# Two weight slots filled once ahead of the experts, and 4 MB loads from the third pair of experts on

## The reference, cut to what matters

```python
def moe(h, w_router, b_router, w_gate, b_gate, w_up, b_up, w_down, b_down):
    logits = (t @ w_router + b_router).astype(jnp.float32)
    top_v, top_i = lax.top_k(logits, TOP_K)
    ...
    for e in range(N_EXPERTS):
        gate = jnp.minimum(t @ w_gate[e] + b_gate[e], SWIGLU_LIMIT)
        up = jnp.clip(t @ w_up[e] + b_up[e], -SWIGLU_LIMIT, SWIGLU_LIMIT)
        hid = (up + 1.0) * gate * jax.nn.sigmoid(gate * SWIGLU_ALPHA)
        y = y + comb[:, e:e + 1] * (hid @ w_down[e] + b_down[e]).astype(jnp.float32)
```

## Time and profile before

| | us |
|---|---|
| three runs | 1310.83, 1312.16, 1315.89 |
| median | 1312.16 |
| span of the profiled execution | 1309.2 |
| TensorE busy in it | 1268.5 |

### The profile page before, as it was taken

One profiled execution on the slowest core, in us unless ns is written; L12 is line 12 of the kernel. 1 busy time (PEld: TensorE's weight loads), 2 busy tenths in 40 slices (PEclk: granted clock), 3 DMA queues, 4 the chain that ended last, 5 costly groups with the idle time before them and its releaser, 6 DMA issues.

```text
span 1309.2 us, 18733 instructions
## 1 busy us (share of the span) xinstructions
PE 1268.5 (97%) x8160; PEld 623.4 (48%) x8160; DVE 412.6 (32%) x836; ACT 192.1 (15%) x353; POOL 16.8 (1%) x38
## 2 busy tenths in 40 slices
PE   9999999999999999999999999999899999999996
PEld 7778765677763443434434343433334343443332
DVE  4987745433122122131222212122122212122122
ACT  4114322221121010000100000010000000010002
POOL 0002000000000000000000000000000000000000
PEclk9999999999999999999999999999999999999998
DMA  9335041495989999999999999999999999999995
GB/s 320 129 111 133 4 138 59 161 377 227 421 323 412 427 428 426 429 427 429 429 429 435 430 432 432 429 430 430 432 430 433 433 433 433 433 433 432 423 427 197
DMA packets 33955, 464.41 MB, mean 355 GB/s; under 512 B 7824, under 2 KB 9424, under 8 KB 13024
## 3 DMA queue, kind: packets, MB, share of 16 engines
q1 hardware_dynamic: 33056, 459.53, 84.3%
q0 software_dynamic: 832, 3.90, 0.9%
HBM read 458.34 MB, written 5.07 MB: 354 GB/s over the span
## 4 chain that ended last, share of the span: by engine, by line
PE 75%; DMA 22%; DVE 2%; ACT 1%; issue 0%; SPq 0%; DVEq 0%
PE ps L1191 37%; PE ps L613 25%; DMA arena<-in_w_down 10%; DMA ring<-in_w_down 9%; PE ps L1222 4%; PE ps L1267 2%; DMA ring<-in_w_gate 2%; PE ps L1218 1%; PE ps L1204 1%; PE ps L1210 1%; DVE ring L1600 0%; DMA ring<-in_w_in 0%; PE ps L1312 0%; PE ps L1255 0%; PE ps L1269 0%
## 5 line engine op out<-in xcount | busy, mean ns | idle before, releaser
L1191 PE MATMUL ps<-ring,xT 128*64 128x512 f32 x1536 | 341.7, 595 | 2.0 <-DMA ring<-in_w_gate 1.3
L613 PE MATMUL ps<-arena,ring 128*128 128x288 f32 (+3 forms) x1136 | 225.3, 366 | 1.2 <-DMA ring<-in_w_in 1.1
L1191 PEld LDWEIGHTS ps<-ring,xT 128*64 128x64 f32 x1536 | 106.2, 137 | 227.2 <-issue 217.3
L613 PEld LDWEIGHTS ps<-arena,ring 128*128 128x128 f32 (+1 forms) x1136 | 176.6, 177 | 47.5 <-issue 4.7
L1191 PE MATMUL ps<-ring,arena 128*64 128x512 f32 x768 | 171.7, 596 | 7.7 <-DMA ring<-in_w_down 7.7
L1355 ACT ACTIVATE arena<-ps 128x512 f32<-128x512 f32 (+5 forms) x136 | 76.4, 570 | 634.4 <-PE ps L1210 367.3
L1191 PE MATMUL ps<-arena,xT 128*64 128x512 f32 x512 | 114.7, 595 | 0.0
L1191 PEld LDWEIGHTS ps<-ring,arena 128*64 128x64 f32 x768 | 52.9, 137 | 108.5 <-issue 97.9
L2063 DVE TENSOR_TENSOR arena<-arena,ps 128x512 f32<-128x512 f32 x64 | 44.0, 688 | 130.2 <-PE ps L1267 117.3
L2015 DVE TENSOR_TENSOR xT<-ps,vec 128x1024 f32<-128x1024 f32 x15 | 18.4, 1225 | 177.7 <-PE ps L1222 177.7
L1191 PE MATMUL ps<-arena 128*64 128x512 f32 x256 | 61.5, 624 | 11.5 <-DMA arena<-in_w_down 11.5
(11 more groups left out here) (227 smaller groups left out, 771.9 us busy)
## 6 DMA issues: line engine op xcount, KB each, us to landing
ring<-in_w_up SPq DMA_DIRECT2D x18, 4096.0 KB, 29.5
ring<-in_w_up SPq DMA_DIRECT2D x28, 2048.0 KB, 21.9
ring<-in_w_down SPq DMA_DIRECT2D x14, 4096.0 KB, 30.8
ring<-in_w_gate SPq DMA_DIRECT2D x9, 4096.0 KB, 30.2
arena<-in_w_gate SPq DMA_DIRECT2D x9, 4096.0 KB, 29.2
ring<-in_w_down SPq DMA_DIRECT2D x16, 2048.0 KB, 20.1
ring<-in_w_gate SPq DMA_DIRECT2D x14, 2048.0 KB, 21.4
arena<-in_w_gate SPq DMA_DIRECT2D x14, 2048.0 KB, 24.9
```

The lines of the kernel that those rows point to most:

```text
L613: return nc.tensor.matmul(out, lhsT, rhs, start=start, stop=stop)
L1191: last = nc.tensor.matmul(out[AT[h ^ swap], :], lhs(k), part(weights(i), 0, 4, D)[:, k % 4, h * 512:(h + 1) * 512], start=(fresh and k == ...
```

## The change

Eight slots stay in turn, and two more, 8 and 9, are placed at the end of a longer `arena`. They take the first two loads of the first pair and are not refilled with weights. Each other load keeps its number; as `FIRST_SLOT` goes, load L stands in slot L % 8. [...] The four large conv stores are issued in two halves each. The matrix whose loads are cut into pieces in the first pair is n = 5 in place of n = 4, and the pieces follow product 1. `small` keeps two biases; the rest is `small_later`, in the second pair, behind `up_done` 2. `WHOLE` becomes 1: loads of 4 MB from the third pair on, and the down biases are added there.

```diff
-WHOLE = 3
+WHOLE = 1
...
-FIRST_SLOT = 2
+ONCE = 2
...
-    return (FIRST_SLOT + load) % SLOTS, load // SLOTS
+    return load % SLOTS, load // SLOTS
+
+
+def place_first(n, c):
+
+    load = 2 * n + c
+    return (SLOTS + load, 0) if load < ONCE else place(0, n, c)
...
+LATER_FILLS = [f - (i < ONCE) for i, f in enumerate(FRONT_FILLS)]
...
-        arena = sb("arena", [P, 23224])
+        SPARE = 27096 - ONCE * SLOT
+        arena = sb("arena", [P, 27096])
...
-            last_front = [("wo_ps", 4), ("wo_ps", 8)] + [("sv_ps", n + 1) for n in range(4)] + [("sv_ps", 4), ("o_out", XH)]
+            last_front = [("wo_ps", 4), ("wo_ps", 8)] + [("sv_ps", n + 1) for n in range(4)] + [("sv_ps", 4), ("o_out", XH)] + [("sk_ps", 4)] * ONCE
 
             def small():
+                for dst, name in ((b_gate, "b_gate"), (b_up, "b_up")):
+                    sp.dma_start(dst, A[name]).then_inc(S["ext_ld"], 16)
+
+            def small_later():
+                sp.wait_ge(S["up_done"], 2)
+                sp.dma_start(b_down, A["b_down"]).then_inc(S["ext_ld"], 16)
                 sp.dma_start(gf_row, A["g_final_row"].broadcast_to([P, D])).then_inc(S["ext_ld"], 16)
                 for d in range(4):
                     sp.dma_start(gf_tail[TAIL * d:TAIL * (d + 1)], A["g_final_row"][:, 256 * d:256 * (d + 1)].broadcast_to([TAIL, 256])).then_inc(S["ext_ld"], 16)
-                for dst, name in ((b_gate, "b_gate"), (b_up, "b_up"), (b_down, "b_down")):
-                    sp.dma_start(dst, A[name]).then_inc(S["ext_ld"], 16)
...
                 for n, (w, p) in enumerate(MATRICES):
+                    if second and n == 2:
+                        small_later()
                     for c in range(2):
-                        i, fill = place(odd, n, c)
-                        if first and fill == 0:
+                        i, fill = place_first(n, c) if first else place(odd, n, c)
+                        if first and n < 5:
                             sem_, val = last_front[i]
                             sp.wait_ge(S[sem_], val)
-                        elif not (first and n == 4):
+                        elif not first:
...
-                        elif first and n == 4:
+                        elif first and n == 5:
                             for k in range(4):
                                 if k < 3:
                                     sp.wait_ge(S["first_k"], 3 * c + k + 1)
+                                elif c == 0:
+                                    sp.wait_ge(slot_free[i], emptied(odd, n, c)[1])
                                 else:
-                                    sp.wait_ge(slot_free[i], emptied(odd, n, c)[1])
+                                    sp.wait_ge(S["up_done"], 1)
...
-            experts(1, 1, 0, 1)
-            with sp.Fori(1, WHOLE) as t:
-                for odd in range(2):
-                    experts(2 * t + odd, 2 * t + odd, t, odd)
+            experts(1, 1, 0, 1, second=True)
...
-                pool.dma_start(O["conv"][:, c, 1:, :],
-                               ext[:, c, TAPS - 1 + SEQ:].rearrange("p (b t) -> p b t", b=NB)[:, :, NT:]).then_inc(S["conv_sent"], 16)
+                for b in range(0, NB, NB // 2):
+                    pool.dma_start(O["conv"][:, c, 1 + b:1 + b + NB // 2, :],
+                                   ext[:, c, TAPS - 1 + SEQ:].rearrange("p (b t) -> p b t", b=NB)[:, b:b + NB // 2, NT:]).then_inc(S["conv_sent"], 16)
...
-                    if opening and n == 0 and k % 4 < 3:
+                    if opening and n == 1 and k % 4 < 3:
                         last.then_inc(S["first_k"], 1)
...
-    nc = bacc.Bacc("TRN2", target_bir_lowering=False, num_devices=1)
+    nc = bacc.Bacc("TRN2", target_bir_lowering=False, num_devices=1, dynamic_dma_scratch_size=1024)
```

More of the change, by code:

```diff
@@ L93, in halves_left_out @@
     return (PAIRS // 2 - 1 - WHOLE) * sum(per_pair) + per_pair[0]
+LATER_FILLS = [f - (i < ONCE) for i, f in enumerate(FRONT_FILLS)]
 FREED = [sum(frees(n, c) for odd in range(2) for n in range(6) for c in range(2) if place(odd, n, c)[0] == i)
          for i in range(SLOTS)]
+UNFREED = [sum(frees(load // 2, load % 2) for load in range(ONCE) if load == i) for i in range(SLOTS)]
 def emptied(odd, n, c):
@@ L106, in emptied @@
         at = 6 * odd + n - 4
-        return "slot_free", sum(frees(m, c) for o, m in loads if 6 * o + m <= at) + (0 if at >= 0 else 0)
+        return "slot_free", sum(frees(m, c) for o, m in loads if 6 * o + m <= at) - UNFREED[i]
     done = "up_done" if n_was in (1, 3) else "down_done"
@@ L169, in weights @@
         def weights(i):
-            return ring[:, i * SLOT:(i + 1) * SLOT] if i < RING else arena[:, (i - RING) * SLOT:(i - RING + 1) * SLOT]
+            if i < RING:
+                return ring[:, i * SLOT:(i + 1) * SLOT]
+            at = (i - RING) * SLOT if i < SLOTS else SPARE + (i - SLOTS) * SLOT
+            return arena[:, at:at + SLOT]
         def whole_slot(i):
@@ L191, in build @@
         shift_out = sb("shift_out", [P, RW, 1 + NB])
-        amax = sb("amax", [P, 9])
-        asum = sb("asum", [P, 9])
+        amax = const[:, 1230:1239]
+        asum = const[:, 1240:1249]
         hT = part(arena, 0, KT, TOK)
@@ L228, in build @@
         sq_tail = arena[:, 10496:10752]
[L229 to L233, removed]
+        gf_row = arena[:, SPARE:SPARE + D]
+        b_gate = arena[0:NE, 13056:14080]
+        b_up = arena[NE:2 * NE, 13056:14080]
+        b_down = arena[0:NE, SPARE + D + 256:SPARE + 2 * D + 256]
+        gf_tail = arena[:, SPARE + D:SPARE + D + 256]
         h_tail = arena[0:2 * TAIL, 14080:14592]
@@ L240, in build @@
         combT = arena[0:NE, 18240:18528]
[L241 to L244, removed]
+        one_e = part(arena, 12928, 2, CAP)[0:2 * NE]
+        pick = part(arena, 10752, TT, 2, CAP)
+        wpick = part(arena, 11136, TT, 2, 2, CAP)
+        ye = (arena[:, 11904:12416], arena[:, 12416:12928])
         after_x = xT[:, :, :].rearrange("p k t -> p (k t)")
@@ L248, in build @@
         y_out = (after_x[:, 2048:3072], after_x[:, 0:1024])
[L249 to L254, removed]
+        w_r = part(arena, 18528, KT, NE)
+        b_r = const[:, 640:672]
+        logit = part(const, 672, TT, NE + TOPK)
+        top8 = part(const, 780, TT, 8)
+        others = part(const, 804, TT, NE + TOPK)
+        dummy = eps[:, 2:3]
         dummy_ln = part(scratch, 13550, 1)
         sqsum = arena[:, 14336:14336 + TOK]
[L257 to L263, removed]
+        mask = part(const, 912, TT, NE)
+        comb = part(const, 1008, TT, NE + 2)
+        pos = part(const, 1110, TT, NE + 2)
+        esum = const[:, 1212:1215]
+        ntop = const[:, 1215:1218]
+        ssq = const[:, 1218:1221]
+        sqx = part(arena, 10752, KT, TOK)
         rstd = ssq
-        load = arena[:, 19856:19857]
-        sq_half = arena[:, 19812:19816]
-        sq_bias = arena[:, 19816:19818]
+        load = const[:, 1221:1222]
+        sq_half = const[:, 1222:1226]
+        sq_bias = const[:, 1226:1228]
         load_i = sb("load_i", [P, 1], I32)
@@ L440, in experts_whole, with experts @@
                     sp.dma_start(whole_slot(i), src).then_inc(slot_in[i], 16)
-            def experts(q, s, u, odd, first=False, last=False):
+            def experts(q, s, u, odd, first=False, second=False, last=False):
                 for n, (w, p) in enumerate(MATRICES):
+                    if second and n == 2:
+                        small_later()
                     for c in range(2):
-                        i, fill = place(odd, n, c)
-                        if first and fill == 0:
+                        i, fill = place_first(n, c) if first else place(odd, n, c)
+                        if first and n < 5:
                             sem_, val = last_front[i]
                             sp.wait_ge(S[sem_], val)
-                        elif not (first and n == 4):
+                        elif not first:
                             done, val = emptied(odd, n, c)
@@ L511, in rounds @@
             later = whole or step
[L512 to L515, removed]
+            if not whole:
+                with eng.Fori(1, PAIRS // 2 - 1) as t:
+                    for odd in range(2):
+                        step(0, 2 * t + odd, 2 * t + odd, t, odd)
+            else:
                 for odd in range(2):
@@ L1176, in product @@
                 for k in ks:
-                    i, fill = place(odd, n, k // 4)
-                    landed = 16 * (fill + 1 + FRONT_FILLS[i]) - (16 * halves_left_out(i) if after and k < 4 else 0)
+                    i, fill = place_first(n, k // 4) if opening else place(odd, n, k // 4)
+                    landed = 48 if i >= SLOTS else 16 * (fill + 1 + LATER_FILLS[i]) - (16 * halves_left_out(i) if after and k < 4 else 0)
                     if pieces and k % 4 < 3:
@@ L1274, in multiply @@
                 def multiply(*args, **kinds):
```

(6 more changed lines are left out.)

19 lines of the change are left out of this document (11 added, 8 removed).

## The result

| | median us | runs |
|---|---|---|
| kernel before | 1311.49 | 4 |
| changed kernel | 1330.82 | 4 |

The changed kernel is slower: ratio 1.0154, 95% interval 1.0126 to 1.0182, about 19 to 20 us. Its profiled execution has a span of 1328.9 us, 19.7 more than before. The forecast was 1321 us in a range of 1305 to 1327. It was right that Pool's wait makes the kernel slower; that term was forecast at +8 us and came to more than twice as much, so the time lies outside the range.

A forecast was written before the change was run, and what follows sets the result against it. An unbroken weight stream from load 10's request, plus a fixed tail, was taken to set the end. Slots -1.2, small loads +4.0, 4 MB loads -1.6 and Pool +8 gave +9.2 us: 1321 us, range 1305 to 1327.

The forecast's parts named there:

- Pool's wait: At the conv stores, Pool waits for ring room and delays TensorE behind filled: +8 us, bounds 4.7 and 13.4; chance 0.55.
- TensorE lives off a lead: Expert stage: one unbroken weight stream, starting with load 10's request, sets the end; TensorE has a lead until 690 us.
- The two slots: Start of expert stage: slots 8 and 9 used once let loads 10 and 11 land slightly earlier, -1.2 us (0 to -2.6).
- I had 24.3: Sign in the first pair: loads 10 and 11 landed 24.3 us after product 0's start, 25.5 before.
- The small loads: Final norm's row, tails and down biases moved into the full stream of the second pair: +4.0 us (+1.8 to +5.3).
- the 4 MB loads: Whole-matrix loads from pair 2 to 5 run at 431 in place of 428 GB/s: -1.6 us (0 to -2).
- my sum without Pool: Slots, small loads and 4 MB loads together, without Pool's term: +1.2 us.
- upper bound of 13.4: Conv stores: eight halves one after another at 3.4 us each, Pool's copy ending at 140.8, TensorE +13.4 us late.
- one half store and a bit: Assumed room in Pool's smaller ring, so Pool can't leave its last issue until the earlier stores are gone.
- Pool does not wait: Rival at the conv stores: Pool does not wait, or not past 125 us; sum +1.2, 1313 us; chance 0.30.
- the 9.8 us stay won: Rival: the two early loads' transfers count in full, -7.4 us in all, 1304.8 us; chance 0.15.
- The bubble at the whole requests: Pairs 2 to 5: queue running dry where a request needs both halves free; forecast absent, at most some 2 us.

The follow-up runs named there:

- run 11: Changed kernel with the conv stores issued behind Pool's two copies and 2 MB loads up to the seventh pair; 1312.16 us, ratio 1.0015.
- run 3: Kernel before with only the final norm's row, its tails and the down biases loaded in the second pair; 1312.73 us, ratio 1.0024.
- run 5: Kernel before with the large conv stores in halves and dynamic_dma_scratch_size 2048; 1320.03 us (one execution).
- run 2: Changed kernel with the loop over the conv stores moved behind Pool's two copies that count filled; 1309.52 us, ratio 1.0002.
- run 1: Kernel before with only the large conv stores in halves and dynamic_dma_scratch_size 1024; 1330.51 us, ratio 1.0166.
- run 6: Kernel before with the large conv stores in halves and dynamic_dma_scratch_size left as it was; 1313.11 us (one execution).
- run 4: Kernel before with only 4 MB loads from the third pair on in place of the seventh; 1308.90 us, ratio 0.9997.
- run 7: Changed kernel, conv stores behind Pool's copies, slots 8 and 9 used again for loads 10 and 11, small loads behind product 5; 1307.92 us, ratio 0.9983.
- run 9: As run 7, but with 2 MB loads up to the seventh pair; 1305.05 us, ratio 0.9959.

## Why the prediction was wrong where it was

**Right.** TensorE lives off a lead and the stream of weights sets the end: the 19.2 us by which product 0 is late are there at the end too, in a span 19.7 us longer. The two slots give next to nothing, since loads 10 and 11 are in when they were before, 25.3 us after product 0 in place of 25.5. I had 24.3, because I let the eight pieces land as fast as they did before; the first was asked for 2.6 us earlier, but into a DMA that stood still. By the stretches the same: run 11, which has the slots and the small loads and lacks the 4 MB loads, has a stretch of 841.3, run 3 without the slots 841.5, so the slots are worth 0.1 us where I had 1.2. The small loads cost 3.1 (forecast +4.0), the 4 MB loads gave 1.7 (forecast -1.6). Together 3.1 - 1.7 - 0.1 = +1.3, as my sum without Pool (+1.2); that the sum comes out so is in part luck, since the slots gave less than forecast and the small loads cost less. The changed kernel shows +0.2, because with the small loads in the stream the 4 MB loads gave more, 841.3 - 838.5 = 2.8 us.

**Wrong: one term of the sum, Pool's.** I forecast that Pool waits for room behind its stores and put TensorE's delay at +8 us, between 4.7 and 13.4. It was 17.5, with 2.1 more for the clock, and 19.2 at product 0. My upper bound of 13.4 had the right picture, each half store landing before the next goes out, and I took 8. No run shows the +8 itself: it was my choice between two bounds worked out from landings before the change, and in its place the runs showed the 17.5 us idle and the 2.1 for the clock. That a ring of 1024 bytes holds "one half store and a bit" was an assumption too; the traces then had one half and at most one small store out at each wait. Two things were missing in the bound:

- *The halves go one at a time, and one of them lands late beside a weight fill.* My upper bound had eight halves at 3.4 us. Six of the seven steps went so: the first took 3.6 us, and from 126.50 to the last issue at 142.88 are five steps of 3.3 us. But the second half, and the small store behind it, landed slowly, 6.9 and 6.8 us after issue in place of the 2.5 to 3.2 of the other halves. The fill of a ring slot with `w_mv`, 2 MB of the front's weights, issued at 117.26, was in the DMA at the time. Rows of DMA in the changed kernel, us to landing, of the stores issued at 115.05, 118.61, 119.37, 129.56, and of that fill:

```profile
out_conv<-arena POOLq DMA_DIRECT2D x1, 60.0 KB, 3.2
...
out_conv<-arena POOLq DMA_DIRECT2D x1, 60.0 KB, 6.9
...
out_conv<-arena POOLq DMA_DIRECT2D x1, 15.0 KB, 6.8
...
out_conv<-arena POOLq DMA_DIRECT2D x1, 60.0 KB, 2.7
...
ring<-in_w_mv SPq DMA_DIRECT2D x1, 2048.0 KB, 9.1
```

  That is one step of 7.9 us (118.61 to 126.50) in place of 3.3, hence 4 us above my bound. In run 5 the first wait ends at 126.36 too, with a ring twice as large and the same fill beside it, where a half took 9.4 us. The landing of 14.7 us that the fill had before was in the trace that I read, and the store that took 9.5 us beside it stood in my rows; I took both for the stores' own slowness. Run 2 takes the fill away: the same eight halves with the same ring go out from 145.31 on, long after the fill has landed, no half that Pool waits for takes more than 3.1 us, and no wait is longer than 3.0. It moves the stores and not the fill, so other work beside them changed too; with the slow landings in three traces, each with the fill, it leaves little doubt that the fill is the cause.
- *The standing still has a price of its own.* After 17 us idle TensorE came back at a granted clock of 0.50 for over 4 us, and the same products took 2.1 us longer. I passed the delay on one to one. The third group of products is 19.7 us late; the half us less at product 0 is within what the front differs by between executions.

That makes 13.4 + 4.0 + 2.1 = 19.5 us. The largest part of the error is a third thing: I chose the middle between two bounds, where my own condition (one half store and a bit) spoke for the upper one, and that alone is 5.4 us of it: if one half is out at a time, each has to land before the next, whatever the average drain. So it went at all seven waits of the changed kernel.

**The rivals.** "Pool does not wait" is refuted by runs 1 and 6, "the 9.8 us stay won" by run 2. The bubble at the whole requests, which I had put at 2 us and found absent, is absent in the changed kernel, 1.0 us in run 4, which has no small loads in the stream, and 3.9 us when the stream starts 9 us earlier (run 7).

## What to carry to other kernels

Setting `dynamic_dma_scratch_size` to 1024 made Pool wait at seven issues that had been free, 20.9 us in all, each time until its stores had landed, and the time 1.5% longer; the same waits cost nothing (18.6 us, ratio 1.0002) once the stores stood behind the copies for which TensorE stands. So look at what stands behind the stores on that engine, and try the stores behind it. Two slots filled once, with loads 10 and 11 in 25.3 us after product 0 and 25.5 before, were worth 0.1 us (run 11 against 3); the same slots used again, with load 10 asked for 9.4 us earlier, 7.7 (run 9 against 11, with the place of the small loads): ask for each load by which earlier load frees its slot, and at what time. And read the granularity of requests against the backlog: whole matrices gained 3.2 us where the whole request landed after 15.2 us (run 2 against 11) and lost 3.1 where it landed after 12.6 (run 7 against 9).

## What the runs showed of the hardware

- Ahead of its DMA issues Pool stood still for 2.0 to 6.7 us per half store, but the first, with `dynamic_dma_scratch_size` 1024 (changed kernel, runs 1 and 2), for 9.0 and 3.1 us with 2048 (run 5), and not at all in twelve stores with it left as it was (run 6). Each of these 23 waits ended 0.3 to 0.4 us after the last of all stores issued so far had landed.
- A store of 60 KB in runs of 120 bytes took 2.5 to 3.7 us from issue to landing with 1024 bytes (changed kernel, runs 1 and 2), and 6.9 and 7.2 us where a 2 MB fill of another queue was in the DMA the whole time (changed kernel, run 1).
- TensorE came back from 17.5 us idle at a granted clock of 0.50 from 145 to 149 us, and was at 1.00 from 150 on. The products at the return took 2.1 us longer; it was 2.7 us after 18.9 us idle (run 1) and 1.7 after 8.6 (run 5).
- From 540 to 700 us loads of 4 MB ran at 431 GB/s (changed kernel, run 7) and of 2 MB at 428 to 429 (kernel before, run 9). Over four pairs the whole difference was 1.7 us (run 4) to 3.2 us (run 2 against 11).
